# A hybrid decoder layer on one core: the fifth norm moved ahead of the second transposes, and one state addition moved behind the last split of the output projection's input

## The reference

```python
n = rmsnorm(h, g_mix)
q, k, v, qi, ki, wi, qb, kb, vb, gb, rb, uc, vc = split_proj(n @ w_in)
q, k = rmsnorm(q, q_norm_g), rmsnorm(k, k_norm_g)        # per head of 128
o_a = attention over the top-k keys that the indexer (qi, ki, wi) selects
o_b, s_b = gla(qb, kb, vb, log_a, state)                 # gated linear attention
o_c = gelu(uc) * (w_spatial @ rmsnorm(gelu(vc)) + b_spatial)
h = h + concat(o_a, o_b, o_c) @ w_out
h = h + (silu(n2 @ w_ffn_gate) * (n2 @ w_ffn_up)) @ w_ffn_down    # n2 = rmsnorm(h)
h = h + sigmoid(rmsnorm(h) @ w_ple_gate) * (p_l @ w_ple_proj)
```

## Time and profile before

| | |
|---|---|
| median of 3 runs | 1400.65 us (1400.3 to 1400.87) |
| the profiled execution's own time | 1400.19 us |
| its span, first to last instruction | 1398.5 us |
| granted TensorE clock, mean over the span | 1.000 |
| PE busy | 1388.0 us (99%), 10750 matmuls |
| DVE busy | 852.0 us (61%) |
| ACT busy | 582.0 us (42%) |
| POOL busy | 123.3 us (9%) |
| from HBM / to HBM | 231.48 MB / 4.47 MB, mean 169 GB/s |

### The profile page before, as it was taken

How to read it: one execution, slowest core, us unless ns; L and a number is a source line. 1 busy time by engine, 2 the same in 40 slices (tenths; PEclk the granted TensorE clock), 3 DMA queues, 4 the chain that set the end, 5 groups by cost and what they waited for, 6 DMA issues and landing times.

```text
span 1398.5 us, 28621 instructions
## 1 busy us (share of the span) xinstructions
PE 1388.0 (99%) x10750; PEld 1371.3 (98%) x10750; DVE 852.0 (61%) x1172; ACT 582.0 (42%) x702; POOL 123.3 (9%) x183
## 2 busy tenths in 40 slices
PE   8999999999999999999999999999999999999999
PEld 8999989999999999999999999999999999999999
DVE  7768777757876555555554445555555556667554
ACT  7446754665334333333333333333333333335332
POOL 1323105001222000000000000000000001112000
PEclk9999999999999999999999999999999999999999
DMA  8757434436544454454545555544544445556553
GB/s 299 211 166 234 164 125 151 141 133 222 194 164 164 167 165 165 162 167 158 177 134 165 165 162 190 168 162 165 165 163 166 159 130 164 162 163 201 179 160 117
DMA packets 76424, 236.72 MB, mean 169 GB/s; under 512 B 13832, under 2 KB 14488, under 8 KB 75992
## 3 DMA queue, kind: packets, MB, share of 16 engines
q1 hardware_dynamic: 71568, 223.56, 49.3%
q0 software_dynamic: 3776, 11.54, 2.6%
q10 hardware_dynamic: 1032, 0.95, 0.2%
HBM read 231.48 MB, written 4.47 MB: 169 GB/s over the span
## 4 chain that ended last, share of the span: by engine, by line
PE 96%; DVE 1%; ACT 1%; DMA 1%; issue 1%; SPq 0%; DVEq 0%; ACTq 0%
PE acc L498 31%; PE acc L500 30%; PE acc L499 30%; DMA proj<-in_xT 1%; PE px L1501 0%; PE px L1617 0%; PE px L1579 0%; PE px L498 0%; PE px L500 0%; PE px L499 0%; DVE w_lo L449 0%; PE px L1560 0%; PE px L1686 0%; PE px L1572 0%; PE px L1459 0%
## 5 line engine op out<-in xcount | busy, mean ns | idle before, releaser
L449 DVE TENSOR_TENSOR w_lo<-w_raw,w_hi 128x1024 fp32r<-128x1024 f32 (+3 forms) x446 | 509.1, 1147 | 312.7 <-ACT w_hi L443 304.4
L443 ACT ACTIVATE w_hi<-w_raw 128x1024 fp32r<-128x1024 f32 (+3 forms) x446 | 439.5, 988 | 552.4 <-PE acc L500 545.6
L498 PE MATMUL acc<-n_hi,w_hi 128*128 128x288 f32 x1664 | 492.5, 296 | 0.0
L499 PE MATMUL acc<-n_lo,w_hi 128*128 128x288 f32 x1664 | 490.9, 295 | 0.0
L500 PE MATMUL acc<-n_hi,w_lo 128*128 128x288 f32 x1664 | 489.2, 294 | 0.0
L500 PEld LDWEIGHTS acc<-n_hi,w_lo 128*128 128x128 f32 x1664 | 313.5, 188 | 0.0
L499 PEld LDWEIGHTS acc<-n_lo,w_hi 128*128 128x128 f32 x1664 | 312.4, 188 | 0.0
L498 PEld LDWEIGHTS acc<-n_hi,w_hi 128*128 128x128 f32 x1664 | 311.8, 187 | 0.0
L498 PE MATMUL acc<-x_hi,w_hi 128*128 128x288 f32 x816 | 245.9, 301 | 0.0
L499 PE MATMUL acc<-x_lo,w_hi 128*128 128x288 f32 x816 | 240.8, 295 | 0.0
L500 PE MATMUL acc<-x_hi,w_lo 128*128 128x288 f32 x816 | 240.0, 294 | 0.0
(11 more groups left out here) (297 smaller groups left out, 867.6 us busy)
## 6 DMA issues: line engine op xcount, KB each, us to landing
w_raw<-in_w_gu SPq DMA_DIRECT2D x176, 512.0 KB, 3.8
w_raw<-in_w_in SPq DMA_DIRECT2D x76, 512.0 KB, 4.3
w_raw<-in_w_down SPq DMA_DIRECT2D x64, 384.0 KB, 3.1
w_raw<-in_w_down SPq DMA_DIRECT2D x64, 320.0 KB, 3.0
w_raw<-in_w_ple SPq DMA_DIRECT2D x32, 576.0 KB, 3.8
w_raw<-in_w_out SPq DMA_DIRECT2D x32, 512.0 KB, 4.3
w_raw<-in_w_in SPq DMA_DIRECT2D x12, 256.0 KB, 6.0
proj<-in_cache_k POOLq DMA_DIRECT2D x16, 128.0 KB, 3.9
```

The lines of the kernel that those rows point to most:

```text
L443: nc.scalar.activation(whi[:, slot, 0:kt * P], raw[:, slot, 0:kt * P], ACT.Copy).then_inc(S("w_hi_done"), 1)
L449: nc.vector.tensor_tensor(wlo[:, slot, 0:kt * P], raw[:, slot, 0:kt * P], whi[:, slot, 0:kt * P].bitcast(F32), ALU.subtract).then_inc(S("w ...
L498: nc.tensor.matmul(out, w_h, row_of(m_hi_, k0 + k), start=first and k == 0, stop=False)
L499: nc.tensor.matmul(out, w_h, row_of(m_lo_, k0 + k), start=False, stop=False)
```

## The change

Two edits. In the timetable's list for half 43, `norm 4` stands ahead of `transpose 1`. And VectorE no longer adds the second half of the new states at half 80: the stage `state_s` does so only for half 0, and the addition for half 1 stands behind the loop that splits parts 1 to 3, in front of the output projection's loop. TensorE's products for it (L1766) stay where they were.

```diff
--- before.py
+++ after.py
@@ -99,7 +99,7 @@
     40: [("mix", 0)],
     41: [("softmax", 1), ("norm_sq", 4)],
     42: [("exps", 1)],
-    43: [("transpose", 1), ("norm", 4), ("pick_s", (8, 9))],
+    43: [("norm", 4), ("transpose", 1), ("pick_s", (8, 9))],
     44: [("mix", 1)],
     45: [("softmax", 2)],
     46: [("exps", 2), ("keys_s", 0)],
@@ -1308,6 +1308,10 @@
                 V.tensor_tensor(s0[half], s0[half], new, ALU.add)\
                     .then_inc(S("state_s_ready"), 1)
 
+            def first_state(half):
+                if half == 0:
+                    state_s(0)
+
             def spatial(_):
                 dve.wait_ge(S("sp_gm"), 1)
                 V.tensor_tensor(gsum[:, :, 0:SEQ].rearrange("p g (c t) -> p g c t", c=2),
@@ -1327,7 +1331,7 @@
             stages = dict(weights=weights, bias_table=bias_table, index=index, index_end=index_end, pick=pick, pick_s=pick_s, norm_sq=norm_sq, norm=norm,
                           softmax=softmax, exps=exps, gate=gate, scan=scan, level=level, level_s=level_s, last=last,
                           decayed=decayed, keys_s=keys_s, softmax_s=softmax_s, mix_s_back=mix_s_back, outputs=outputs,
-                          keys_i=keys_i, scale_q=scale_q, state_s=state_s, first_rows=first_rows,
+                          keys_i=keys_i, scale_q=scale_q, state_s=first_state, first_rows=first_rows,
                           gelu_u=gelu_u, out_scale=out_scale, spatial=spatial)
             for half in range(FIRST_STAGE, 2 * N_IN):
                 if half % 2:
@@ -1344,6 +1348,7 @@
                 if c == 1:
                     split_lo(dve, "in", 0, 2 * N_IN - 1 + NSLOT)
                     gelu_u(3)
+            state_s(1)
 
 
             def one(ap, m):
```

## The result

| | median | lowest to highest | runs |
|---|---|---|---|
| before | 1400.84 us | 1400.07 to 1401.87 | 22 |
| changed | 1402.85 us | 1401.02 to 1404.47 | 22 |

The ratio is 1.0015, with a 95% interval of 1.0009 to 1.0021: 2.0 us slower, 1.3 to 2.9 by the interval. The forecast was 1400.05 us within 1399.0 to 1401.9, so the time lies outside the range and on the other side. The profiled execution of the changed kernel took 1404.44 us, one of the slowest of its 22. Its trace shows the mechanism well, but at more than its median size.

The account below looks back on a forecast made before the run. TensorE bounds the kernel, busy 1388.0 of 1398.5 us, with only 1.30 us of waits to regain. Gains of 0.23 and 0.37 us bring the span to 1397.9 and the median from 1400.65 to 1400.05 us, range 1399.0 to 1401.9.

Parts of the forecast that it names:

- First part: Half 43: norm matmuls moved into TensorE's wait ahead of the second transposes, L1579 at 173.83 instead of 174.06, gain 0.23 us.
- a drain at the two table loads: ScalarE at half 43: page's drain of about 1.38 us beside each load, costing some 2.5 us; chance 0.01.
- Second part: State addition behind the splits: TensorE's wait for L1037 goes, 0.52 us, less 0.15 for a late store, gain 0.37 us.
- VectorE did not hold it up: Store issue beside the w_lo split: page's port rule could delay it up to 0.85 us; not counted.
- the term for the store: Second half's state store, ahead of the first addition into h: takes 3.3 us, lands at 343.0, 0.15 us late.
- My high end: State store's upper bound: 4.3 us like the 512 KB weight loads, landing at 344.0, second part then -0.63 us.
- The two rows of the same kind of store: The two existing state stores in the profile before, 2.9 and 10.8 us; the slow one queued behind the load of h.
- slower, by the store alone: First addition into h: late store costs TensorE each microsecond, 1403.55 us at 6.8 us; chance 0.08 for 1 to 3 us late.
- a store later still: State store landing more than 1 to 3 us late, the very late store counted as slower; chance 0.05.
- the point where the cover ends: State store landing at 343.58, 3.9 us after its issue, uses up both gains; every further microsecond is TensorE's.
- The gate: Output projection: TensorE waits for the second w_lo split, restarting 4.16 us after the first addition into h starts, no slack.
- my cases: Chances: gain of 0.3 to 1.2 us 0.60, nothing moves 0.25, late store 0.08 and 0.05, ScalarE drain 0.01, faster 0.01.

Follow-up runs that it names:

- the norm alone: Only norm 4 moved ahead of transpose 1 in half 43, made to the kernel before: 1400.75 us, ratio 1.0000.
- the state alone: Only the second state addition moved behind the last split, made to the kernel before: 1402.91 us, ratio 1.0013.
- both edits and the wait put off: Changed kernel, with VectorE waiting for the third state store from its second output-projection round on, not the first: 1399.78 us, ratio 0.9993 to the kernel before.

## Why the prediction was wrong

- **First part, +0.23 us: right in its steps.** The mixing matmul was forecast at 173.83 with a wait of 0.29 us for L850. It is issued at 174.02, in a trace that stood 0.17 us later at half 43 (168.79 - 0.13 against the 168.49 of the earlier trace rows, 0.14 of it from the launch), so at 173.85 on the clock of before. The issue ahead of it is at 173.57, which leaves a wait of 174.02 - 173.57 - 0.13 = 0.32 us. ScalarE's chain ran as worked out, without a drain at the two table loads (the first starts at 169.02 behind L443's end at 169.01, and the logarithm 0.01 us behind the load). Of the 0.21 us by which L1584 comes earlier, 0.1 goes again at the restart behind the new wait: the next matmul follows 0.53 us behind it and not 0.43. The gain is of a size that no run can tell from nothing, as the norm alone shows.
- **Second part, 0.52 us for L1037: right.** The wait is gone, and it gave 0.63 us with its restart. L1308 stood behind the third split, at 338.91, in a trace that stood 0.7 us later by then (the products of the first tile ended at 343.49, forecast 342.83). The issue beside the `w_lo` split took 0.54 us, as before, and the first packet went 1.12 us after it, against 1.11 for the first store of the same trace, beside which VectorE ran nothing; so VectorE did not hold it up.
- **The step that failed** is the term for the store: "I take 3.3 us, nearer to the free one, because the stretch of full DMA load ends there: landing at 343.0, 0.15 us late". It took 5.8 us in the changed kernel, landed 2.76 us late, and took 4.6 to 6.9 us in the others that sent it whole beside the weight stream. The load of h had drained, as I said (it landed 0.6 us ahead of the issue), but the output projection's weight stream and an instruction fetch were in flight on the same engines. The table of steps shows the share of each, one execution a row. My high end, the 4.3 us of the weight loads, was too low. This one term, 3.3 against 5.8 us, is 2.5 of the 2.8 us by which the median missed the forecast. The two rows of the same kind of store (2.9 and 10.8) were the bounds to keep. I narrowed them by an argument on what else was in flight, without reading which transfers were.
- **The rival "slower, by the store alone"** was the right one. It priced 6.8 us at 1403.55; 5.8 to 6.6 us came out at 1402.85 to 1402.91. I gave it 0.08 and, for a store later still, 0.05. Its price, one for one from the point where the cover ends, is what the table of gaps shows.
- **The gate was nearer than I wrote.** I let TensorE wait for the second split 4.16 us behind the first addition. It waits for the addition itself, whose accumulator tile (1,0) takes next: it restarts 0.13 us after L1360's end. Before, L1355 ended at 343.88 + 0.45 = 344.33 and the matmul was issued on time at 344.79: 0.33 us of cover. Both gates charge a late store one for one, so the sum did not fail on it.
- **The half clock was in none of my cases.** In the profiled execution it added 1.6 us to the 2.6 of the gap. The median would not need it: 1400.84 less the gains of 0.1 and 0.63 plus a gap of 2.6 is 1402.7, against 1402.85. The profiled executions, 1404.44 here and 1406.4 with the state alone, show it. Of the 22 runs of the changed kernel the eight slowest, from 1403.59 us on, have a mean granted clock of 0.999 in seven cases, and the other fourteen in one; so it fits that about a third of the executions had such a stretch.

What stays open: how far the landing varies among executions of one kernel, since a profile shows one of them, and why the fetch falls there. Every kernel traced has it, between 341.16 and 343.99 us, the kernel before at 342.70 for 0.93 us, where the store had landed by 342.66. With the second edit the store is in flight when the fetch comes. The fetch would fit TensorE's code as it enters the output projection's loop, but no run tested that.

The experiments point to the version with both edits and the wait put off: 1399.78 us, 3.1 us under the changed kernel's median and 0.9 under the one before. The second difference has an interval up to 1.0002 and is not established.

## What to carry to other kernels

When an instruction moves, the DMA behind it moves too; look for every wait on that DMA's landing, and ask which of them protects memory that is written so soon. Putting off the one wait that didn't took back the whole loss, 3.1 us on the medians; in the kernel before, where the store was in time, it gave nothing. Where a landing becomes the last thing to come, bound it by the slowest like transfer in the trace and not by the quiet one: here it ended with the last of 16 shares, up to 2.0 us behind the fifteenth. And price a TensorE stall of some microseconds at more than its length: behind the gaps of 2.61 and 3.53 us the clock fell here, for another 1.6 and 1.4 us.

## What was not expected of the hardware

- The granted clock fell to 0.50 behind gaps of 2.61, 3.38 and 3.53 us in an otherwise gapless stretch, for 3.41, 6.83 and 3.41 us. It did not behind gaps of 2.26 and 2.45 us. These are five single executions.
- A 16 KB instruction fetch took 0.93 to 1.95 us at this place. Where it took 1.67 and 1.95 us, one sixteenth of a 512 KB store landed 2.0 and 1.9 us behind the other fifteen.
- TensorE's wait that the profile calls `issue` (L1741) ended 0.09 us after a DMA landed, in the changed kernel at 297.82.
- The first matmul after a wait for a semaphore is followed 0.1 us later than one without a wait (0.24 against 0.13 us at L1037, 0.53 against 0.43 at L1584), so here a wait that went away gave about 0.1 us on top of its length.
